# Half of a merge's gate products, moved from the merge into the slots of the attention head before it

## The reference, cut to what matters

```
def merge_branches(o_gla, o_ret, m_gla, m_ret, w_branch_gla, w_branch_ret, w_out):
    y = sigmoid(m_gla) * (o_gla @ w_branch_gla) + sigmoid(m_ret) * (o_ret @ w_branch_ret)
    return y @ w_out

def mixer_heads(h, w_in, ...):
    (gq, gk, gv, gg, glr_f, glr_b, rq, rk, rv, rg, m_gla, m_ret) = split_columns(h @ w_in)
    ...
    o_f, s_gf = gla_scan(gq, gk, gv, log_gate(glr_f, 0), states[0], False)
    o_b, s_gb = gla_scan(flip(gq), flip(gk), flip(gv), flip(log_gate(glr_b, 1)), states[1], True)
    o_gla = rmsnorm(o_f + flip(o_b), gla_norm) * silu(heads(gg, GLA_HEADS))
```

## Time and profile before

| | |
|---|---|
| median of 3 runs | 4169.73 us (4164.83 to 4170.53) |
| the profiled execution | 4167.81 us, its span 4165.7 us |
| PE busy | 3900.9 us, 94% of the span |
| DVE, ACT, POOL busy | 1752.9, 1386.0 and 713.9 us |
| mean granted clock of PE | 0.97 of full |

### The profile page before, as it was taken

How to read it: one execution, slowest core, us unless ns; L and a number is a source line. 1 busy time by engine, 2 the same in 40 slices (tenths; PEclk the granted TensorE clock), 3 DMA queues, 4 the chain that set the end, 5 groups by cost and what they waited for, 6 DMA issues and landing times.

```text
span 4165.7 us, 44632 instructions
## 1 busy us (share of the span) xinstructions
PE 3900.9 (94%) x16066; PEld 2128.2 (51%) x16066; DVE 1752.9 (42%) x3686; ACT 1386.0 (33%) x3382; POOL 713.9 (17%) x904
## 2 busy tenths in 40 slices
PE   7999899999999999999999988999999999958995
PEld 3444466655444556555466565446556544423331
DVE  2543576354253565363456554013222201343445
ACT  3433555133233554243344534112222312111113
POOL 1021000032011000130234333002221101012331
PEclk9999999999999999999999999999999999979997
DMA  4101210022111231121010020101110110159885
GB/s 201 41 1 44 99 52 24 31 87 71 54 41 46 107 116 41 53 87 66 21 34 12 17 90 22 41 15 40 41 43 28 46 41 31 69 238 375 322 312 226
DMA packets 88167, 346.24 MB, mean 83 GB/s; under 512 B 20984, under 2 KB 52864, under 8 KB 69136
## 3 DMA queue, kind: packets, MB, share of 16 engines
q1 hardware_dynamic: 69520, 304.55, 19.6%
q0 software_dynamic: 18432, 38.85, 2.6%
HBM read 400.91 MB, written 37.83 MB: 105 GB/s over the span
## 4 chain that ended last, share of the span: by engine, by line
PE 84%; DVE 5%; ACT 4%; issue 3%; DMA 3%; POOL 1%; SPq 0%; POOLq 0%; DVEq 0%; ACTq 0%
PE psum L88 41%; PE psum L94 8%; PE psum L1604 6%; PE psum L2050 5%; PE psum L3243 4%; PE psum L942 4%; PE psum L919 4%; PE psum L3265 2%; PE psum L2277 2%; DMA arena<-hn_scratch,arena 1%; PE psum L319 1%; PE psum L2234 1%; PE psum L1441 1%; PE psum L1981 1%; DVE arena L175 1%
## 5 line engine op out<-in xcount | busy, mean ns | idle before, releaser
L88 PE MATMUL psum<-arena 128*128 128x512 f32 (+4 forms) x4704 | 1817.0, 544 | 40.6 <-DVE arena L2790 13.6
L88 PEld LDWEIGHTS psum<-arena 128*128 128x128 f32 (+1 forms) x4704 | 877.7, 189 | 908.9 <-issue 816.7
L94 PE MATMUL psum<-arena 128*128 128x128 f32 (+2 forms) x3024 | 442.8, 280 | 49.8 <-DMA arena<-hn_scratch,arena 8.8
L94 PEld LDWEIGHTS psum<-arena 128*128 128x128 f32 (+2 forms) x3024 | 343.5, 142 | 252.5 <-issue 165.5
L2050 PE MATMUL psum<-arena 128*128 128x512 f32 (+1 forms) x640 | 287.2, 577 | 8.7 <-DVE arena L2078 5.0
L1604 PE MATMUL psum<-arena 128*128 128x512 f32 x576 | 260.0, 600 | 0.9 <-ACT arena L1736 0.9
L3243 PE MATMUL psum<-arena 128*64 x512 | 232.6, 608 | 21.7 <-issue 10.8
L3244 PE MATMUL psum<-arena 128*64 128x512 f32 x512 | 232.6, 608 | 0.0
L175 DVE SCALAR_TENSOR_TENSOR arena<-psum,arena 128x512 f32<-128x512 f32 (+1 forms) x100 | 60.5, 605 | 404.4 <-ACT arena L172 404.4
L170 ACT ACTIVATE arena<-psum 128x512 f32<-128x512 f32 (+1 forms) x100 | 52.9, 529 | 489.7 <-PE psum L88 489.7
L942 PE MATMUL psum<-arena 64*128 64x512 f32 (+1 forms) x800 | 167.6, 550 | 21.3 <-ACT arena L1032 13.5
(11 more groups left out here) (395 smaller groups left out, 4900.0 us busy)
## 6 DMA issues: line engine op xcount, KB each, us to landing
arena<-w_gu SPq DMA_DIRECT2D x32, 2048.0 KB, 8.8
arena<-w_ada SPq DMA_DIRECT2D x24, 2048.0 KB, 8.0
arena<-w_dn SPq DMA_DIRECT2D x32, 1024.0 KB, 7.7
arena<-w_in SPq DMA_DIRECT2D x12, 2048.0 KB, 8.7
arena<-w_out SPq DMA_DIRECT2D x6, 2048.0 KB, 8.0
arena<-gate_rows_scratch SPq DMA_DIRECT2D x36, 256.0 KB, 3.4
x_scratch<-arena SPq DMA_DIRECT2D x18, 512.0 KB, 3.1
arena<-x SPq DMA_DIRECT2D x16, 512.0 KB, 10.8
```

Of the source, the lines that this page charges most:

```text
L88: ins = e.matmul(out, l, r, start=(i == 0), stop=(i == n - 1))
L94: ins = e.transpose(o, i, idn)
```

## The change

- PE does the eight gate products of the merge's first half (g = 0) in head 3's slots, quarter by quarter (`pe_gla_bgm`): tiles 0, 1, 2, 3, 4, 5 and 7 in slots 4 to 31, tile 6 in slots 40 to 43. The banks are 2 and 7 in turn, which the projections of the other heads use, and bank 6 for tile 6.
- ACT copies six of the results, as they are, into buffers of SBUF that are free by then (`a_gla_bgm`, `raw_z`), each at the head of the slot that follows the tile's last quarter. Tiles 6 and 7 stay in PSUM, in the banks where the merge looks for them.
- The merge leaves these eight products out, and ACT and DVE read the six copies in their place (`merge_z`).
- The weights of both products of g = 0 are loaded in head 2, between the stores, instead of after them. The order of `wseq` changes so that the gate weights of g = 1 go into the buffer which those of g = 0 leave, and the first retention weights into that of the branch weights.

```diff
-        wseq += [(n, g) for g in range(2) for n in ("bg", "bgm")]
-        wseq += [(n, h) for h in range(4) for n in ("ret", "rg")]
+        wseq += [("bg", 0), ("bgm", 0), ("bg", 1), ("ret", 0), ("bgm", 1), ("rg", 0)]
+        wseq += [(n, h) for h in range(1, 4) for n in ("ret", "rg")]
...
+        AT_BGM = [(4 + 4 * i + q, f, q) for i, f in enumerate((0, 1, 2, 3, 4, 5, 7)) for q in range(4)]
+        AT_BGM += [(40 + q, 6, q) for q in range(4)]
+        AT_BGM_COPY = [8 + 4 * f for f in range(6)]
+        raw_z = [Sb[:, 0, 2 * f:2 * f + 2, :].rearrange("p a b -> p (a b)") for f in range(4)] + [LRT[:, 512 * f:512 * f + 512] for f in range(2)]
...
+                    if c == NC_T and h == 2:
+                        load_w(e, ("bg", 0), I["w_bg"][0], 512, proj.of("gla", 2, NT - 1))
+                    if c == NC_T + 4 and h == 2:
+                        load_w(e, ("bgm", 0), I["w_bg_m"][0], 512, proj.of("gla", 3, NT - 1))
...
+        def bgm_bank(t):
+            return P[6] if t == 6 else P[2 if t % 2 and t < 7 else 7]
+
+        def pe_gla_bgm(e, t, q):
+            w = weight(("bgm", 0), 512)
+            if q == 0:
+                if t < 2:
+                    e.wait_ge(*w_ready(("bgm", 0)))
+                    e.wait_ge(*vcop.of("gla", 3, NT - 1 - t))
+                elif t == 6:
+                    e.wait_ge(*acop.of("gg", 3, 3))
+                else:
+                    e.wait_ge(*acop.of("bgm", 4 if t == 7 else t - 2))
+            for k in (2 * q, 2 * q + 1):
+                ins = e.matmul(bgm_bank(t), xnT_2[:, k, tile(NC_T + t)], w[:, k, :], start=(k == 0), stop=(k == 7))
+            if q == 3:
+                ins.then_inc(*proj.by("merge_m", "bg", 0, t))
+
+        def a_gla_bgm(e, t):
+            e.wait_ge(*proj.of("merge_m", "bg", 0, t))
+            e.wait_ge(*prod.of("gla_o", 2, NT - 1))
+            e.activation(raw_z[t], bgm_bank(t), ACT.Copy).then_inc(*acop.by("bgm", t))
...
         def sp_merge(e, name):
...
+            if name == "bg":
+                all_met(e, ("gla",))
+                load_w(e, ("bg", 1), I["w_bg"][1], 512, proj.of("gg", 3, NL_T - 1))
+                load_w(e, ("bgm", 1), I["w_bg_m"][1], 512, proj.of("merge_m", "bg", 0, 6))
+                return
...
-                    if g == 0 or t >= 2:
+                    if (g == 0 and name == "br") or (g and t >= 2):
                         merge_m(e, name, g, t)
...
+        def merge_z(name, n):
+            return raw_z[n] if name == "bg" and n < 6 else P[4 + n % 4]
...
-                   (proj.of("merge_m", "bg", 0, 7), proj.of("merge_m", "bg", 1, 7), proj.of("rg", 0, NT - 1),
+                   (proj.of("merge_b", "bg", 0, 7), proj.of("ret", 0, NT - 1), proj.of("rg", 0, NT - 1),
                     proj.of("rg", 1, NT - 1))[h])
```

More of the change, by code:

```diff
@@ L2380, in pe_gla @@
                     pe_gla_tile(e, h, *divmod(q, 4))
+                for s, t, i in AT_BGM:
+                    if g == 3 * SLOTS + s:
+                        pe_gla_bgm(e, t, i)
                 for h, i in due(g, AT_GG):
@@ L2403, in a_gla @@
             for g in gla_slots():
+                for t, s in enumerate(AT_BGM_COPY):
+                    if g == 3 * SLOTS + s:
+                        a_gla_bgm(e, t)
                 for h, f in due_next(g, NEXT_TILE):
@@ L2480, in sp_merge @@
         def sp_merge(e, name):
[L2481 to L2489, removed]
+            if name == "bg":
[3 more added lines that the diff above has]
+                return
+            load_w(e, ("br", 0), I["w_br"][0], 512, proj.of("rg", 2, NT - 1))
+            load_w(e, ("brm", 0), I["w_br_m"][0], 512, proj.of("ret", 3, NT - 1))
+            load_w(e, ("br", 1), I["w_br"][1], 512, proj.of("rg", 3, NT - 1))
+            load_w(e, ("brm", 1), I["w_br_m"][1], 512, proj.of("merge_b", "br", 0, 7))
         def merge_free(e, name, n):
@@ L2529, in a_merge @@
                     e.wait_ge(*(vmul if name == "bg" else gmul).of("merge", name, n - 2))
-                a_log1p(e, sg2[:, t % 2, :], P[4 + n % 4]).then_inc(*aexp.by("merge", name, n))
+                a_log1p(e, sg2[:, t % 2, :], merge_z(name, n)).then_inc(*aexp.by("merge", name, n))
                 e.wait_ge(*vsta.of("merge", name, n))
@@ L2538, in v_merge @@
                 e.wait_ge(*aexp.of("merge", name, n))
-                v_logsig(e, s, P[4 + n % 4], s).then_inc(*vsta.by("merge", name, n))
+                v_logsig(e, s, merge_z(name, n), s).then_inc(*vsta.by("merge", name, n))
                 e.wait_ge(*aexp.of("merges", name, n))
```

## The result

The changed kernel takes 4133.39 us (median of 4 runs, 4128.45 to 4135.84), the kernel before 4168.70 us in the same comparison (4164.83 to 4170.53). The ratio is 0.9919, 95% interval 0.9908 to 0.9931: faster by 35.3 us. The forecast was 4141, with a range of 4136 to 4155.

A forecast was written before the change was run, and what follows sets the result against it. PE bounds the kernel (84% of the chain), with 27.2 us of gaps in head 3. Terms -55.0 - 1.0 + 1.7 + 10.4 + 13.7 + 1.4 = -28.8 gave 4139.0, or 4141 for the median; range 4136 to 4155.

The forecast's parts named there:

- slots 4 to 20: Head 3: 16 quarters plus 15.3 us of PE work make 42.8, plus 1.5 for waits, 44.3 against 33.9: +10.4 us.
- slots 20 to 32: Head 3: 11 quarters, 18.9 us, added to 27.3 busy, plus 1.0 for waits, give 47.2: +13.7 us.
- slots 40 to 44: Head 3's tail: four quarters, 6.9 us, mostly hidden in waits, PE 1.5 late at a transposition: +1.4 us.
- the merge, with its start: Merge: eight products leave a stretch without gaps, -55.0 us; 1.0 of 1.7 lost to half clock at its start returns.
- rival 1: Head 3's slots go at head 2's pace, no gain at the merge's start: -20.4 us, 4149; chance 14%.
- Copies: Six ACT copies in slots 4 to 32, 3.6 us in all, cost nothing; uncovered, at most 22 us.
- Gate weights: Before slot 4: issued about 2467.7, landing at 2475.8, PE there at 2476.40; cost nothing, up to 1 us.
- The rule weighed: Slots 4 to 20: sustained work keeps PE's clock up, as the sum assumes; if the array goes cold first, 4150.
- half clock: Array goes cold in gaps of slots 0 to 4, first slots run long: 8.5 us lost, 4150; chance 7%.
- late weights: Gate weights come late, PE stands at slot 4 until 2487.5: 11 us, 4152; chance 6%.
- the chain over the copies: Slots 4 to 32: late quarter delays copy, exponential, L2213 and PE; old gaps stay, slower, 4191; chance 4%.
- The fifth: Merge doesn't get shorter, being bound by the sigmoids; only the slots' growth counts: about 4170; chance 3%.

The follow-up runs named there:

- four tiles: Changed kernel with only gate tiles 0 to 3 inserted, in slots 4 to 19, and tiles 4 to 7 back in the merge: 4144.91 us.
- eight quarters: Changed kernel with only gate tiles 0 and 1 inserted, spread over slots 5 to 14, the rest back in the merge: 4146.64 us.
- loads alone: Changed kernel's new order of loads and buffers, with all gate products back in the merge: 4166.17 us, 0.9997 of the kernel before.

## Why the prediction was off

The mechanism was right: PE's gaps in head 3 took up the products, and PE's work set the length of the filled slots. Sizes in the sum were off. It was 5.5 us too small, against mark to mark, and these are its terms:

| | forecast | measured |
|---|---|---|
| slot 4's quarter | +1.7 | +1.7 |
| slots 4 to 20 | +10.4 | 42.83 - 33.92 = +8.9 |
| slots 20 to 32 | +13.7 | 44.33 - 33.52 = +10.8 |
| slots 32 to 40 | 0 | 18.18 - 18.65 = -0.5 |
| slots 40 to 44 | +1.4 | 13.03 - 11.68 = +1.3 |
| the merge, with its start | -56.0 | 165.94 - 222.57 = -56.6 |
| sum | -28.8 | -34.3 |

**The step that failed** is "PE is at full clock here, so 27.3 + 18.9 = 46.2, plus 1.0 for waits". The term was +13.7 and measured +10.8: 1.9 us too much work and 1.0 for waits of which none stayed. The busy time of a stretch holds the way of the last record before each wait through the array. In a stretch with gaps this counts as busy, though the next group could have followed; in a full one it is hidden. Rows of the kernel before show it:

```profile
2514.48 1.89 PE L2277 MATMUL psum<-arena 128*128 128x256 f32 x8
2517.54 1.13 PE L2234 MATMUL psum<-arena 128*128 128x128 f32 x8 [1.17 <-issue]
2518.51 0.60 PE L2150 MATMUL psum<-arena 128*128 128x256 f32 x2
```

The first group is busy 1.89 us for 1.73 of work, and the one after the wait takes 0.97 from start to start where 0.89 is its work. Seven such waits and the slow starts behind them make 27.30 out of 25.4. Counted with the prediction's own times per record, the kernel before alone gives 25.4 us for this stretch, so the number could be had without a run. I had counted so in slots 4 to 20, and didn't do it in slots 20 to 32. The runs show the same: PE's work was 44.33 - 11 x 1.72 = 25.4 us, and the room 8.1 us and not 6.2. Three tiles alone, in these slots only, gave the same 44.3. The low end of the range went by the same 27.3: "all gaps closed" was set at -32.0, and with 25.4 it would have been -33.9, or 4136 for the median. So the measured time was outside what I had called the limit. The last 2.4 us down to 4133.39 are 0.4 by the marks (34.3), 1.0 because the kernel before took 4168.70 in this comparison and not 4169.73, and 1.0 by which the medians differ more than the marks.

**Slots 4 to 20.** The count was right to 0.1 us (42.8 against 42.83). The 1.5 us for waits that stay were wrong: none stayed, in this kernel or with four tiles. Head 2's 3.4 us were no model, as rival 1 itself hinted: 2.8 of them are its projection quarters waiting for DVE, which copies the next head's transposed keys and queries out of their bank. With only eight quarters (15.3 + 13.8 = 29.1 us of work) the loop of POOL and ACT, 33.6 us, is the bound again, so it is the larger of the two that counts, not their sum.

**Merge.** 55.0 for eight products was right. Its start at half clock had cost 1.6 us, and the whole of it came back, not the 1.0 that I took.

**Tail.** +1.3 as worked out. That the tail itself can fall to half clock was missed; without tile 6 the tail came out at 13.47 us and not 11.7.

**What was costed at nothing.** Copies: right, and with six times as many 1.3 us in all. Loads: right, 329.87 against 329.64 us mark to mark. Gate weights: they fit, with 0.7 us to spare, as forecast (2475.8 for the landing). The price of late ones was too low, since the 7.61 us wait of the kernel with a later load cost 2.7 us more at half clock. The median fell by 35.3 and the marks by 34.3; the difference is within the spread of the runs.

**The rule weighed.** Quarters from slot 4 on did keep the clock up: 1.00 in the changed kernel, 1.00 also with four tiles and with eight quarters, 0.75 to 0.76 in the three kernels without quarters there (the one before, loads alone, three tiles). The late weights' 3.58 us for a quarter of 1.72 show the clock at half after a wait of 7.61 us. The Trainium skill (TensorE: Matmul & The Clock Gate, Part 1) says that the array is cold, at half clock, by default and after idling, and this trace agrees. The tail is another case: PE wasn't idle in it but thinly filled, and it fell to half clock in some profiles and not in others. In slots 4 to 20 of the kernel before, half clock cost nothing, since with eight quarters and at full clock the stretch was only 0.3 us shorter.

**The rivals.** Head 2's pace fell with four tiles, half clock with the changed kernel's own clock, late weights with its slot 4, the chain over the copies with six of them. The fifth fell with the merge's 165.94 us. Its time did not follow from its own terms either: with the merge as long as before and 27.2 us of growth in the slots it would have been 4169.7 + 27.2, about 4197, and not 4170. (The 27.2 us of gaps at the start of the prediction are 27.1 by the rows.)

What stays open: whether tile 6 keeps the tail's clock up in every execution. It did in all seven profiles that have it there, but no run fills the tail with other work, and the executions without a profile don't tell. Whether the quarters could as well stand behind the scores of their slots, and not ahead, was not tried.

## What to carry to other kernels

Work of a saturated stretch that depends on nothing near it is worth, moved into a stretch with gaps, the gaps it fills: here 55.0 - 22.7 = 32.3 of the 34.3 us, the rest being the clock at the merge's start and 0.5 in slots 32 to 40. Count the target's work from distances between starts, not from busy time, and take the larger of that work and the pace of the other engines. With the quarters ahead of what used to wait, no allowance for waits was needed here. Then spread the pieces: none where the engine is already full, some in each slot that waits. A buffer that comes free earlier opens more gaps; here that was worth 1.7 us, and the better spread 1.8 more.

## What the runs showed of the hardware

- The same thinly filled tail (5.0 of 11.7 us busy) ran at full clock in two profiles and partly at half in four (7.2 of 13.5 us busy in one), and with the merge's start that cost 1.7 to 5.3 us. Which of the two levels such a stretch gets differs between executions of the same instructions there, so such a term needs a range.
- A wait of 7.61 us at the head of a full stretch cost 10.3 us: the array came back at half clock, with 3.58 us for a quarter of 1.72.
- Taking 4 MB of loads out of a stretch (DMA share 0.55 to 0.26) changed nothing for the engines that compute in it: 33.92 and 34.09 us.
